# First layer of a two-block transformer kernel: x turned ahead, the eight column tiles summed as 2, 2, 2, 1, 1

## The reference

```python
c_act = jax.nn.silu(c)
shift, scale, gate = jnp.split(c_act @ mod_w[i] + mod_b[i], 3, axis=-1)
h = _rms_norm(x, norm_g[i]) * (1.0 + scale[:, None, :]) + shift[:, None, :]
y = _retention(h, positions, w_in, w_out)      # i = 0: h @ w_in, 1024 x 6144
...
q, k, v, g, f = jnp.split(h @ w_in, ...)       # i = 1: f has 16 columns, the forget gates
x = x + gate[:, None, :] * y
```

## Time and profile before

| | before |
|---|---|
| median of 3 runs | 696.29 us (696.11 to 696.35) |
| the profiled execution | 696.31 us, span 694.5 us |
| PE, DVE, ACT busy | 98%, 72%, 55% of the span |
| granted TensorE clock | 1.00 throughout |
| DMA, first 50 us | about 350 GB/s; after 60 us a mean of 187 GB/s |

### The profile page before, as it was taken

One profiled execution on the slowest core, in us unless ns is written; L12 is line 12 of the kernel. 1 busy time (PEld: TensorE's weight loads), 2 busy tenths in 40 slices (PEclk: granted clock), 3 DMA queues, 4 the chain that ended last, 5 costly groups with the idle time before them and its releaser, 6 DMA issues.

```text
span 694.5 us, 11561 instructions
## 1 busy us (share of the span) xinstructions
PE 679.4 (98%) x4591; PEld 553.8 (80%) x4591; DVE 499.8 (72%) x803; ACT 381.3 (55%) x561; POOL 17.3 (2%) x35
## 2 busy tenths in 40 slices
PE   7889999999999999999999999999999999999996
PEld 4669997777878888888788877778878888888885
DVE  4788998787986779766768889777665555565445
ACT  5447434565655666554665765845574444444444
POOL 4011000000000000000000000000000000000000
PEclk9999999999999999999999999999999999999999
DMA  9999875667897176833455654433756666655511
GB/s 298 369 377 341 313 247 175 199 225 246 284 350 219 38 243 234 272 124 101 148 153 155 190 171 129 147 122 117 210 160 212 181 188 180 197 185 189 185 60 60
DMA packets 74405, 138.81 MB, mean 200 GB/s; under 512 B 5732, under 2 KB 18400, under 8 KB 74352
## 3 DMA queue, kind: packets, MB, share of 16 engines
q1 hardware_dynamic: 72816, 134.92, 60.4%
q10 hardware_dynamic: 736, 1.81, 0.7%
q0 software_dynamic: 800, 1.35, 0.6%
HBM read 137.01 MB, written 1.05 MB: 199 GB/s over the span
## 4 chain that ended last, share of the span: by engine, by line
PE 88%; DVE 5%; ACT 2%; SPq 2%; DMA 1%; issue 1%; DVEq 0%; ACTq 0%
PE G L392 23%; PE G L394 22%; PE G L393 22%; PE T L433 4%; PE G L412 2%; PE G L413 2%; PE G L414 2%; DVE wlo L1119 2%; PE T L791 2%; DMA arena<-in_mod_w_dram 1%; PE T L779 1%; DVE arena L1128 1%; SPq L2552 1%; SPq L2540 1%; ACT whi L1932 1%
## 5 line engine op out<-in xcount | busy, mean ns | idle before, releaser
L1119 DVE TENSOR_TENSOR wlo<-raw,whi 128x1024 fp32r<-128x1024 f32 x202 | 245.6, 1222 | 111.1 <-ACT whi L1932 110.6
L1932 ACT ACTIVATE whi<-raw 128x1024 fp32r<-128x1024 f32 x202 | 212.2, 1061 | 130.7 <-PE G L394 89.2
L392 PE MATMUL G<-whi,ahi 128*128 128x512 f32 x694 | 280.4, 404 | 0.2 <-DVE wlo L1119 0.2
L394 PE MATMUL G<-whi,alo 128*128 128x512 f32 x694 | 271.0, 391 | 0.0
L393 PE MATMUL G<-wlo,ahi 128*128 128x512 f32 x694 | 270.4, 390 | 0.0
L392 PEld LDWEIGHTS G<-whi,ahi 128*128 128x128 f32 x694 | 130.3, 188 | 29.4 <-issue 1.8
L394 PEld LDWEIGHTS G<-whi,alo 128*128 128x128 f32 x694 | 130.2, 188 | 28.3
L393 PEld LDWEIGHTS G<-wlo,ahi 128*128 128x128 f32 x694 | 130.6, 188 | 25.4 <-issue 1.0
L1934 ACT ACTIVATE arena<-T,st 128x128 f32<-128x128 f32 (+2 forms) x56 | 21.9, 478 | 30.0 <-DVE st L1525 30.0
L1932 ACT ACTIVATE ahi<-T 128x512 fp32r<-128x512 f32 x25 | 15.0, 600 | 39.5 <-PE T L433 39.5
L1934 ACT ACT_TABLE_LOAD x27 | 34.6, 1283 | 3.3 <-issue 1.8
(11 more groups left out here) (254 smaller groups left out, 626.5 us busy)
## 6 DMA issues: line engine op xcount, KB each, us to landing
raw<-in_ret_w_in_dram SPq DMA_DIRECT2D x48, 512.0 KB, 6.4
raw<-in_w_gate_up_dram SPq DMA_DIRECT2D x40, 512.0 KB, 3.8
raw<-in_mod_w_dram SPq DMA_DIRECT2D x32, 512.0 KB, 4.7
raw<-in_fox_w_in_dram SPq DMA_DIRECT2D x32, 512.0 KB, 4.7
raw<-in_w_in_dram SPq DMA_DIRECT2D x28, 512.0 KB, 3.8
raw<-in_w_down_dram SPq DMA_DIRECT2D x22, 512.0 KB, 3.5
arena<-in_mod_w_dram SPq DMA_DIRECT2D x16, 512.0 KB, 9.3
raw<-in_ret_w_out_dram SPq DMA_DIRECT2D x16, 512.0 KB, 5.6
```

What stands on the lines that cost most here:

```text
L392: e.matmul(o, ah, wh, start=first and k == 0, stop=False)
L394: done = e.matmul(o, al, wh, start=False, stop=last and k == 1)
L1119: e.tensor_tensor(o, a, b, op).then_inc(sig[name], 1)
L1932: d = e.activation(o, a, f, scale=scale)
```

## The change

- `SUMMED` becomes (0, 1), (2, 3), (4, 5), (6), (7); `VECTOR_ROWS` is 5 for all.
- x is turned ahead: four `turn_x0(b)`, two tiles each, into the banks G0 to G3 before the first sums; ScalarE copies them to a new buffer `xT` (`x0_copy`), which lies over the positions' buffer. `x0_high(k)` makes ahi from xT in one activation, and VectorE makes the full value in stage0 itself (`x0_full`), before `x0_low`.
- The sums have banks of their own, T2 for k = 0 to 3 and T3 for 4 to 7; a group signals once.
- SyncE's order: group 0 in two parts ahead of item 0; group 1 in parts ahead of items 2 and 3; group 2 ahead of 5 and 6; group 3 ahead of 8; group 4 ahead of 10.
- GpSimd's wait ahead of the positions is for `x0` 8 (alo of k = 7). The load `dec` on ScalarE waits for the same.
- The forget product takes high and low weights as one set of 32 columns (two matmuls a k), and the turn behind it adds the two by a matmul with the selection matrix.

```diff
-SUMMED = [(0,), (1,), (2, 3), (4, 5), (6, 7)]
-VECTOR_ROWS = [4, 4, 6, 6, 6]
+SUMMED = [(0, 1), (2, 3), (4, 5), (6,), (7,)]
+VECTOR_ROWS = [5, 5, 5, 5, 5]
...
+        xT = region(11776, 2048).rearrange("p (k n) -> p k n", k=8)
+        def columns_made(g):
+            return sum(2 * len(ks) + 1 for ks in SUMMED[:g]) + len(SUMMED[g]) + 1
...
             def sums_at(k, a):
-            return (G[a] if k == 0 else T[a] if k == 1 else T[2 + k % 2])[:, 256 + 32 * a:256 + 32 * a + 32]
+            at_ = 64 * (k % 4) + 32 * a
+            return T[2 + k // 4][:, at_:at_ + 32]
...
             def shift_scale(g):
...
+                for i in range(len(SUMMED[g])):
                     for a in range(2):
                         own_rows(g, i, a)
+                for i in range(len(SUMMED[g])):
+                    for a in range(2):
                         d = other_rows(g, i, a)
-                    d.then_inc(sig["sums"], 1)
+                d.then_inc(sig["sums"], 1)
...
+            turn_x0(0)
+            turn_x0(1)
+            keep_warm(3)
+            turn_x0(2)
+            turn_x0(3)
             keep_warm(6)
+            shift_scale(0)
+            keep_warm(6)
+            on_.wait_ge(sig["xn"], 8)
+            for k in range(8):
+                u = 3 * (k // 2) + k % 2
+                if k == 7:
                     rows_unit(u, k)
+                elif k == 6:
+                    rows_unit(u, k, (0,))
+                    shift_scale(4)
+                    rows_unit(u, k, (1,))
+                else:
+                    rows_unit(u, k)
+                if k % 2:
+                    if k == 1:
+                        on_.wait_ge(sig["rows_read"], 3)
+                    products(u + 1, 0, (4, 5, None), k - 1, k == 1, k == 7)
+                    if k < 7:
+                        shift_scale(k // 2 + 1)
+                    products(u + 1, 1, (4, 5, None), k - 1, k == 1, k == 7)
...
             for k in range(8):
-                e.matmul(t[0:16, 0:S], wh, ahi[:, k, :], start=k == 0, stop=False)
-                e.matmul(t[0:16, 0:S], wl, ahi[:, k, :], start=False, stop=False)
-                d = e.matmul(t[0:16, 0:S], wh, alo[:, k, :], start=False, stop=k == 7)
+                e.matmul(t[0:32, 0:S], ahi[:, 29, 32 * k:32 * k + 32], ahi[:, k, :], start=k == 0, stop=False)
+                d = e.matmul(t[0:16, 0:S], narrow[:, k, 0, :], alo[:, k, :], start=False, stop=k == 7)
...
+            def x0_full(k):
+                on_.wait_ge(sig["mod0"], columns_made(group_of[k]))
+                on_.wait_ge(sig["xn"], xT_made(k))
+                on_.wait_ge(sig["x0"], k - 3)
+                ts(stage0[:, k % 4, :], xT[:, k, :], col(AB[:, 0, :], k), col(AB[:, 0, :], 8 + k), ALU.mult, ALU.add, "mod0")
...
+            for g, us in enumerate(((0, 1), (2, 3, 4), (5, 6, 7), (8, 9), (10, 11))):
+                if g:
+                    mod_sums(g, 0, 4)
+                    if g < 4:
+                        ring_to(us[0])
+                    mod_sums(g, 4, VECTOR_ROWS[g])
+                modulated(g)
+                for k in SUMMED[g]:
+                    x0_full(k)
+                ring_to(us[1] if 0 < g < 4 else us[0])
+                for k in SUMMED[g]:
+                    x0_low(k)
+                ring_to(us[-1])
             ring_to(11)
...
+            for g, us in enumerate(((0, 1, 2), (3, 4, 5), (6, 7, 8), (9,), (10, 11))):
+                ring_to(us[0])
+                for k in SUMMED[g]:
+                    x0_high(k)
+                ring_to(us[-1])
             ring_to(12)
...
-            on_.wait_ge(sig["mod0"], 12)
+            on_.wait_ge(sig["x0"], 8)
             e.dma_start(posi, pos_in.partition_broadcast(P).rearrange("p a n -> p (a n)")).then_inc(sig["small_in"], 16)
...
+            before = {0: ((0, 0), (0, 1)), 2: ((1, 0),), 3: ((1, 1),), 5: ((2, 0),), 6: ((2, 1),), 8: ((3, 0),), 10: ((4, 0),)}
```

More of the change, by code:

```diff
@@ L439, in keep_warm @@
                 for _ in range(n):
-                    e.matmul(G[2][:, :], warm[:, 0:P], warm, start=True, stop=True)
+                    e.matmul(T[3][:, :], warm[:, 0:P], warm, start=True, stop=True)
             keep_warm(9)
@@ L463, in x_ready, with turn_x0 @@
                     ready[slot + k0 + k, m] = (sig["x_split"], 4 * p + (2 + 2 * (k // 2) if n < 4 else 1 + k))
[L466 to L470, removed]
+            def turn_x0(b):
+                on_.wait_ge(sig["xn"], 2 if b < 2 else 4)
+                transposes(G[b], [xn0[:, m, k * P:(k + 1) * P] for k in (2 * b, 2 * b + 1) for m in range(2)], "x0_turned")
             def own_rows(g, i, a):
@@ L477, in own_rows @@
                     for c in range(0, P, 32):
-                        e.matmul(o[c:c + 32, :], mod_tile(g)[:, a, r, i * P + c:i * P + c + 32], cact[:, r:r + 1].to_broadcast([P, 32]), start=r == r0, stop=False)
+                        e.matmul(o[c:c + 32, :], mod_tile(g)[:, a, r, i * P + c:i * P + c + 32], cact[:, r:r + 1].to_broadcast([P, 32]),
+                                 start=i == 0 and a == 0 and r == r0, stop=False)
             def other_rows(g, i, a):
@@ L483, in other_rows, with shift_scale @@
                 for c in range(0, P, 32):
[L484 removed]
+                    d = e.matmul(sums_at(SUMMED[g][i], a)[c:c + 32, :], macc[:, g % 2, a, i * P + c:i * P + c + 32], ones[:, 0:32],
+                                 start=False, stop=a == 1 and i == len(SUMMED[g]) - 1)
                 return d
[L487 removed]
+            def shift_scale(g):
                 on_.wait_ge(sig["cact"], 1)
@@ L491, in mod_landed @@
                     on_.wait_ge(sig[f"mod_in{i}"], n)
[L493 to L505, removed]
-                d.then_inc(sig["sums"], 1)
[L507 to L512, removed]
+                for i in range(len(SUMMED[g])):
                     for a in range(2):
                         own_rows(g, i, a)
+                for i in range(len(SUMMED[g])):
+                    for a in range(2):
                         d = other_rows(g, i, a)
-                    d.then_inc(sig["sums"], 1)
-                    summed(k)
+                d.then_inc(sig["sums"], 1)
+                for k in SUMMED[g]:
+                    for m in range(2):
+                        ready[k, m] = (sig["x0"], k + 1)
             def rows_unit(u, k, columns=(0, 1)):
@@ L548, in _ @@
[L548 to L552, removed]
-                    rows_unit(u, k)
[L554 to L561, removed]
+            on_.wait_ge(sig["filled"], 1)
@@ L701, in turn_forget @@
                 on_.wait_ge(sig["forget"], 1)
+                on_.wait_ge(sig["head2_in"], 32)
                 t = bank("forget_t", sig["forget"], 2)
                 for m in range(2):
-                    d = e.transpose(t[:, 16 * m:16 * m + 16], zT[:, m * P:(m + 1) * P], idf[0:16, 0:16])
+                    d = e.matmul(t[:, 16 * m:16 * m + 16], zT[:, m * P:(m + 1) * P], head[0:32, C_SEL:C_SEL + 16], start=True, stop=True)
                 d.then_inc(sig["forget_pe"], 1)
@@ L2545, in _ @@
             for n, (_, srcs, w, *_) in enumerate(items):
-                if n in before:
-                    load_mod(before[n])
+                for g, part in before.get(n, ()):
+                    load_mod(g, part)
                 t = raw_tile(n)
```

113 lines of the change are left out of this document (43 added, 70 removed).

## The result

| | before | after |
|---|---|---|
| median | 696.25 us (696.11 to 696.35, 4 runs) | 708.29 us (706.35 to 710.02, 4 runs) |
| ratio to before | | 1.0172, 95% interval 1.0139 to 1.0206 |
| profiled execution | 696.31, span 694.5 | 710.02, span 708.2 |

The change makes the kernel 1.7% slower, 12.0 us. The prediction had the sign, but 2.4 us of it.

The account below looks back on a forecast made before the run. TensorE, busy for 98% of the span, was taken as the bound, with the first layer's first round moving the end. Late acc loads +3.3 and forget product -0.9 made 696.3 into 698.7 us, range 697.0 to 702.0.

Parts of the forecast that it names:

- The sign and its mechanism: Loads behind GpSimd's later wait stall VectorE, then PE between units 11 and 12; slower by over 0.2%, chance 0.83.
- the sum: Added-up times through the acc loads to unit 16, ready at 74.94 instead of starting at 71.7: net +3.3 us.
- The lengths within the loop: Stages of PE's and VectorE's loop in the first layer's first rounds: 10.8 us a round, against 11.1.
- k = 7's own loop: Last tile's separate group, summed behind k = 6: gives back what the earlier k = 6 wins, first round ending at 60.2.
- T0: Time at which alo of k = 7 is there, releasing GpSimd's wait: 54.6 us.
- The start: Work up to the first unit, longer with group 0 at 2 MB: k = 0 at 18.1, against 14.2 before.
- The first two rounds: From k = 0 to k = 4, 10.8 us each: k = 2 at 28.9, k = 4 at 39.7.
- every stage of the loop has a row: Argument against the rival that the late loads don't decide: the loop's stage times are backed by trace rows.
- The landing: Last mod_b load into acc, issued at 57.3, takes 3.0 us, bounded by 1.9 and 6.3, landing at 60.3.
- the rival B: The mod_b load takes 6.3 us to land, as before: 702.0 us; chance 0.18 for it or the way to it.
- The hold at unit 16: VectorE has unit 16 ready at 74.94, PE is there at 74.24, so PE waits for VectorE.
- The forget product: 24 matmuls become 16, at 0.114 each: 0.9 us less on TensorE; lower bound of the gain 0.

Follow-up runs that it names:

- e2: The kernel before with only GpSimd's wait made late, from the columns of k = 5 to alo of k = 7: 699.35 us, +2.9 to before.
- e1: The changed kernel with GpSimd's wait and the positions load moved behind the two mod_b loads into acc: 701.05 us, +4.6 to before.
- e6: e1 with 64 small matmuls of 32 columns added behind the 16 warming products, to shift PE's instruction list: 699.32 us, +3.2 to before.
- e5: e1 with VectorE summing six of a group's eight rows instead of five: 697.50 us, +1.4 to before.
- e9: e5 with the last two column tiles as one group (2, 2, 2, 2), the split undone: 695.79 us, -0.5 to before.
- e11: The changed kernel with VectorE summing six rows of eight instead of five, nothing else: 704.38 us, +8.1 to before.
- e3: The changed kernel with 25 warming products instead of 16 ahead of the first turn of x: 710.54 us, +14.1 to before.
- e4: The kernel before with only the forget product's part of the change: 695.83 us, -0.6 to before.
- e10: e9 with 25 warming products at the start instead of 16 and the six ahead of group 0's sums removed: 694.72 us, -1.6 to before.
- e7: e6 without the six warming products between the turns of x and the first sums: 702.00 us, +5.9 to before.
- e8: e6 with the last two column tiles as one group (2, 2, 2, 2): 702.31 us, +6.2 to before.
- e12: e10 with SyncE's load order undone, both parts of a group's rows issued together ahead of its first item: 697.53 us, +1.2 to before.

## Where the prediction was right and where it failed

**The sign and its mechanism: right.** GpSimd waits for alo of k = 7, which is there at 62.77; the last mod_b load is issued at 65.43, 2.66 later as the sum has it; and PE's gap lies between unit 11 and unit 12. e2 gives +2.9 for this wait in before, e1 7.4 in after.

**The lengths within the loop: nearly right.** A round without a stop is 11.25 with five rows (e6; 10.8 said), the third 10.2 (9.9), k = 6 to k = 7 5.06 (5.05). The full tile costs 0.41, which is the far bound of the two and not the 0.35 that I chose. The sums of a pair take 1.23, not 1.05: I took the 80 small matmuls of the earlier trace rows, and there are 128. That the early k = 6 is more than given back by k = 7's own loop came out as said; against a pair it costs 2.0 us of unit 12's start (e5 to e9), a comparison that the prediction did not make.

**The failed step: T0, 54.6 said, 62.8 measured.** Of the 11.3 us by which unit 16 was late against the sum (74.94 said, 86.23 measured), 8.2 come in here, in three places.
- The start, 2.8: k = 0 at 20.90 and not 18.1. The clock, which the prediction never considered, was 0.66 from 10 to 15 us behind a pause of PE (9.1 to 11.05). e1, with the same instructions on PE there and a clock of 1.00, starts at 19.38, so 1.5 goes with the clock. Of the other 1.3 some 0.2 is the sums (1.23 for the 1.05 of a pair); the rest I haven't placed.
- The first two rounds, 5.1: 26.74 for them instead of 21.6. By e6 the loop itself is 0.9 of this (22.5); the other 4.2 are the stop of 2.96 us, worth 1.4 by e1, and the clock of 0.50 behind it, worth 2.8. In e5 and e11, which have six rows and no stop, the two take 21.98.
- The third round, 0.3.

The step that the prediction took as sure, "every stage of the loop has a row", left out that PE must have its instructions, and that the clock falls behind a pause of PE. Over the whole profile of after the clock is the largest single part: 1.5 in the start, 2.8 behind the stop and 1.6 behind the gap are 5.9 of the 13.7. I asked of each moved operation what data it waits for and never how many instructions it packs into a microsecond.

**The landing, 3.0 said, 5.1 measured.** The lull that I expected in the DMA queues is there only in part (share 0.54 at 62 to 66 us, 0.89 at 66 to 70). Neither bound was broken, 1.9 and 6.3, but the value was taken too near to the quiet row. e2 measured 3.7 and 4.0 for the two loads, e11 4.4 and 4.9, e3 4.5 and 6.1. This is 2.1 of the 11.3, and the rival B, which would have it at 6.3, was nearer than the forecast.

**The hold at unit 16: wrong, and replaced by another.** The sum had VectorE late at unit 16 by 0.7; PE was late by itself, since after 4.60 us idle the clock fell and units 12 to 16 took 13.03 us instead of the 11.44 of the sum. That is 1.6 more and the 0.7 of the hold less, so +0.9, and 8.2 + 2.1 + 0.9 is 11.2 of the 11.3. The rows of it, PE after the stall, with 0.21 between starts where the earlier trace rows have 0.12:

```profile
73.57 0.42 PE L430 MATMUL G<-alo,whi 128*128 128x256 f32 x1
73.79 0.42 PE L431 MATMUL G<-ahi,wlo 128*128 128x256 f32 x1
...
76.35 0.33 PE L431 MATMUL G<-ahi,wlo 128*128 128x256 f32 x1
```

**The forget product: right**, 0.6 by medians of e4, with the 0.9 in its interval.

**Read as medians**, the 12.0 us go: 7.4 to the wait (e1), 3.2 to the stop and the row that VectorE doesn't do (e5), and 1.4 are left. These 1.4 are 2.0 for the split (e9) and 1.1 for the start (e10), less the 1.6 by which e10 beats before, of which 0.6 is the forget product (e4). All of these differences hold what the clock lost with them.

**What stays open.** The split of the stop's cost, 1.4 by itself and 2.8 by the clock, rests on one profile each of e1, e6 and after. Why the clock stayed at 1.00 behind the same stop in e1 and fell in after and e3 isn't shown; the runs of e1 differ among themselves, so one profile may be chance. Why the packet of a block comes when it does, 2.5 us before PE goes on and not earlier, isn't shown either; the positions are measured, the trigger is not. Nor is it told apart whether e5 has no stop because its bursts are shorter or because its blocks end elsewhere.

## What to carry to other kernels

When a wait is made later, list every instruction behind it in that queue, loads above all, and price the first reader of each: one changed wait cost 2.9 us in a kernel that it touched nowhere else, and moving two small loads ahead of it gave 7.4. When short instructions are packed together on an engine, ask what feeds the engine, and look in the profile for waits with no releaser; if such a wait stays at one count of instructions when work is added before it, or moves by a whole block, the supply is the first thing to suspect. And read the granted clock behind every pause of the engine: what is lost there comes on top of the pause.

## What the runs showed of the hardware

- PE stopped for 1.13 to 4.17 us with no releaser, behind 347 matmuls of its list in after (345 recorded in e1 and e3), behind 221 in e6, e7 and e8, and behind 728 in e8; an instruction packet of 16.5 KB came 2.4 to 2.7 us before it went on.
- The granted clock fell from 2.4 to 1.2 GHz behind pauses of PE of 1.8 us (e2) to 5.6 us (e3), and was at 0.50 from 33.0 to 38.5 us in after; it cost 1.6 us in units 12 to 16 in after and as much in e2. It does not fall each time: in the profiles it stayed at 1.00 behind a pause of 2.88 in e1, of 2.84 in e12 and of 1.83 in e9.
- A load of 4 to 8 KB issued by GpSimd landed after 3.7 to 6.1 us in e2, e3, e11 and after, at DMA shares of 0.5 to 0.9. The Trainium skill (DMA: Bandwidth & Descriptors, section "Anatomy of one DMA — SWDGE (gpsimd) path") has about 2.0 us as its fixed part; the rows here are 1.9 to 3 times that, and only the 1.9 of the earlier trace rows agrees.
